# Three stage boundaries reordered: first rows normalised in halves on two engines, then two weight tiles multiplied chunk by chunk

## What is computed

```
def rmsnorm(x, g):
    xf = x.astype(jnp.float32)
    y = xf * lax.rsqrt(jnp.mean(xf * xf, axis=-1, keepdims=True) + EPS)
    return (y * g.astype(jnp.float32)).astype(x.dtype)

    h = modulate(rmsnorm(x, ffn1_pre_g[l]), m[0], m[1])          # stage ffn1
    y = swiglu(h, ffn1_w_gate[l], ffn1_w_up[l], ffn1_w_down[l])
    x = x + 0.5 * m[2][:, None, :] * rmsnorm(y, ffn1_post_g[l])

    h = modulate(rmsnorm(x, mix_pre_g[l]), m[3], m[4])           # stage mix1
    proj = h @ w_in[l]
    ...
    x = x + m[5][:, None, :] * rmsnorm(y, mix_post_g[l])

    h = modulate(rmsnorm(x, ffn2_pre_g[l]), m[6], m[7])          # stage ffn2
    y = swiglu(h, ffn2_w_gate[l], ffn2_w_up[l], ffn2_w_down[l])
    x = x + 0.5 * m[8][:, None, :] * rmsnorm(y, ffn2_post_g[l])
```

## Time and profile before

| | us |
|---|---|
| median of three runs | 2482.9 |
| the runs | 2482.52, 2482.9, 2487.58 |
| time of the profiled execution | 2484.59 |
| its span in the trace | 2482.8 |
| PE busy | 2442.2 (98% of the span) |
| DVE busy | 1613.1 (65%) |
| ACT busy | 1206.1 (49%) |
| POOL busy | 681.8 (27%) |

### The profile page before, as it was taken

One profiled execution on the slowest core, in us unless ns is written; L12 is line 12 of the kernel. 1 busy time (PEld: TensorE's weight loads), 2 busy tenths in 40 slices (PEclk: granted clock), 3 DMA queues, 4 the chain that ended last, 5 costly groups with the idle time before them and its releaser, 6 DMA issues.

```text
span 2482.8 us, 40495 instructions
## 1 busy us (share of the span) xinstructions
PE 2442.2 (98%) x16435; PEld 2242.0 (90%) x16435; DVE 1613.1 (65%) x3096; ACT 1206.1 (49%) x1828; POOL 681.8 (27%) x326
## 2 busy tenths in 40 slices
PE   8999989999999999999999999999999999999999
PEld 8997869988989999999888888889999999888887
DVE  7777866647556568999444445574676899644444
ACT  5444664446644454434444445664444434444443
POOL 1210001112036560000444443115662000344443
PEclk9999999999999999999999999999999999999999
DMA  9996436654355554444656655335555444556554
GB/s 349 404 336 241 136 111 196 203 195 150 119 165 176 171 179 148 142 139 138 212 191 195 195 192 196 123 115 193 184 170 164 143 137 144 186 189 196 192 195 161
DMA packets 126732, 457.45 MB, mean 184 GB/s; under 512 B 14117, under 2 KB 17105, under 8 KB 125778
## 3 DMA queue, kind: packets, MB, share of 16 engines
q1 hardware_dynamic: 121858, 442.57, 53.6%
q10 hardware_dynamic: 4048, 8.91, 1.1%
q0 software_dynamic: 640, 3.37, 0.4%
HBM read 451.63 MB, written 5.93 MB: 184 GB/s over the span
## 4 chain that ended last, share of the span: by engine, by line
PE 84%; DVE 2%; ACT 1%; POOL 0%; issue 0%; ACTq 0%
PE bank L612 25%; PE bank L614 25%; PE bank L613 25%; PE bank L1199 4%; PE bank L979 1%; PE bank L1170 1%; PE bank L840 1%; DVE sb L1870 0%; PE bank L1122 0%; PE bank L627 0%; ACT sb L1242 0%; PE bank L997 0%; DVE sb L1931 0%; PE bank L829 0%; POOL sb L2783 0%; PE bank L1084 0%
## 5 line engine op out<-in xcount | busy, mean ns | idle before, releaser
L612 PE MATMUL bank<-sb,sb 128*128 128x256 f32 (+1 forms) x4744 | 1518.9, 320 | 12.4 <-DVE sb L1870 4.5
L613 PE MATMUL bank<-sb,sb 128*128 128x256 f32 (+1 forms) x4744 | 1493.5, 315 | 0.0
L614 PE MATMUL bank<-sb,sb 128*128 128x256 f32 (+1 forms) x4744 | 1493.3, 315 | 0.0
L1242 ACT ACTIVATE sb<-sb 128x1024 fp32r<-128x1024 f32 x765 | 809.4, 1059 | 1162.6 <-PE bank L614 1143.5
L1870 DVE TENSOR_TENSOR sb<-sb,sb 128x1024 fp32r<-128x1024 f32 x511 | 628.4, 1231 | 584.8 <-ACT sb L1242 582.4
L2771 POOL TENSOR_TENSOR sb<-sb,sb 128x1024 fp32r<-128x1024 f32 x254 | 623.0, 2454 | 1325.5 <-ACT sb L1242 1321.5
L612 PEld LDWEIGHTS bank<-sb,sb 128*128 128x128 f32 x4744 | 907.8, 191 | 77.1 <-issue 12.6
L613 PEld LDWEIGHTS bank<-sb,sb 128*128 128x128 f32 x4744 | 908.6, 192 | 55.1 <-issue 1.0
L614 PEld LDWEIGHTS bank<-sb,sb 128*128 128x128 f32 x4744 | 907.5, 191 | 55.6
L2735 DVE TENSOR_TENSOR sb<-sb,sb 128x1024 fp32r<-128x1024 f32 x64 | 159.9, 2498 | 149.5 <-ACT sb L1826 149.5
L2698 DVE TENSOR_SCALAR sb<-sb,sb 128x128 f32<-128x128 f32 x512 | 142.5, 344 | 0.0
(11 more groups left out here) (274 smaller groups left out, 1199.7 us busy)
## 6 DMA issues: line engine op xcount, KB each, us to landing
sb<-in_peer_down_dram SPq DMA_DIRECT2D x256, 512.0 KB, 3.3
sb<-in_peer_up_dram SPq DMA_DIRECT2D x256, 512.0 KB, 3.3
sb<-in_w_ada_dram SPq DMA_DIRECT2D x72, 512.0 KB, 7.5
sb<-in_hyb_in_dram SPq DMA_DIRECT2D x56, 512.0 KB, 3.4
sb<-in_ffn_gate_dram SPq DMA_DIRECT2D x44, 512.0 KB, 4.8
sb<-in_ffn_up_dram SPq DMA_DIRECT2D x44, 512.0 KB, 4.6
sb<-in_ffn_down_dram SPq DMA_DIRECT2D x44, 512.0 KB, 4.2
sb<-in_mix_in_dram SPq DMA_DIRECT2D x25, 512.0 KB, 3.4
```

What stands on the lines that cost most here:

```text
L612: e.matmul(out, a[0], b[0], start=start, stop=False)
L613: e.matmul(out, a[0], b[1], start=False, stop=False)
L614: return e.matmul(out, a[1], b[0], start=False, stop=stop)
L1242: self.e.activation(rr(M.hi[k % NSPLIT]), M.raw[k % NRAW], AF.Copy).then_inc(*self.S.tick("hi", k))
```

## The change

It touches the three gated boundaries, and in one detail the order of the transposes everywhere.

- **DVE, `gated_residual`:** the first half of the rows t = 0 is normalised ahead of `times(1, 1)` and `add(1)`; the second half isn't done on DVE any more.
- **ACT, `gated_residual`:** a new `normalise` does that second half in the place of one of the three splits; the first of the later splits follows it. The third split (tile 2) moves: into `shifted`, behind chunk 1, at the entry to mix1 and ffn2; in front of the features at hyb0.
- **ACT and DVE, `shifted`:** for the odd chunks ACT writes `hhi` itself by a second read of the bank; DVE copies only the even ones.
- **`LOWS`:** the low part of tile 1 of mix1 and ffn2 is made by POOL and no longer by DVE.
- **PE, `features`:** the rows t = 0 are transposed in the order 0 to 7 (before: 0, 4, 1, 5, ...), k of 4 and more waiting for ACT's half. At mix1 and ffn2 follows one matmul over a single row, 512 columns, plain float32 (`opened`), which sets the first pair's bank to zero; then the rows t = 1.
- **PE, `first_pair`:** tiles 0 and 1 are multiplied together into that bank: chunks 0 to 3 of tile 0, chunks 0 to 3 of tile 1, then chunk 4 of both, chunk 5 of both, and so on.

```
@@ LOWS
-    "mix1": ((33, ("dve",)),),
+    "mix1": ((1, ("dve",)), (2, ("pool",)), (33, ("dve",))),
@@ Tensor
     def features(self):
...
+        banks = [self.take() for _ in range(4)]
+        for t in range(2):
+            for k in (0, 4, 1, 5, 2, 6, 3, 7) if t else range(8):
+                self.after_rows(t, k)
+                o = 256 * (k // 4) + 128 * t
+                x = self.e.transpose(banks[k % 4][:, o:o + 128], M.xn[:, t, 128 * k:128 * (k + 1)], M.const("ident"))
+                if t and k >= 4:
+                    x.then_inc(*self.S.tick("turned", s, "x", k % 4))
+            if t == 0 and s and shifted:
+                self.first = self.opened()
...
+    def opened(self):
+        M, bank = self.M, self.take()
+        o = M.consts["upto"][0]
+        self.e.matmul(bank, M.const("later")[0:1, :], M.con[0:1, o:o + 512], start=True, stop=False)
+        return bank
+
+    def first_pair(self, name, *freed):
+        M, bank = self.M, self.first
+        self.K.bank[name] = bank
+        tiles = [self.taken() for _ in range(2)]
+        for i, c in [(i, c) for i in range(2) for c in range(4)] + [(i, c) for c in range(4, 8) for i in range(2)]:
+            hi, lo = self.weights(tiles[i])
+            self.after_low(tiles[i])
+            self.wait_ge("h_lo", self.s, "x", c)
+            w = slice(128 * c, 128 * (c + 1))
+            x = self.mm3(bank[:, 256 * i:256 * (i + 1)], (hi[:, w], lo[:, w]), (rr(M.hhi[:, c]), rr(M.hlo[:, c])),
+                         False, i == 1 and c == 7)
+            if c == 7:
+                x.then_inc(*self.S.tick("tile", tiles[i]))
...
@@ Scalar, shifted
-        for dst in (self.m.f[k % 4],) if s else (self.m.f[k % 4], rr(M.hhi[:, k])):
+        for dst in (self.m.f[k % 4], rr(M.hhi[:, k])) if s == 0 or k % 2 else (self.m.f[k % 4],):
@@ Scalar, features
             self.shifted(k)
+            if self.s and k == 1:
+                self.ahead()
@@ Scalar, gated_residual
         square(1, 1)
-        self.split()
+        self.normalise(s + 1)
         self.split()
         self.squares(s + 1, 1)
         self.split()
+    def normalise(self, s):
+        M, c = self.M, slice(512, 1024)
+        self.wait_ge("rstd", s, "x", 0)
+        self.e.activation(M.xn[:, 0, c], M.x[:, 0, c], AF.Copy, scale=self.norm_of(s, "x_r0")).then_inc(*self.S.tick("xn_act", s))
@@ Vector, shifted
         for k in range(8):
             self.wait_ge("feature", s, "x", k)
-            self.e.tensor_copy(rr(M.hhi[:, k]), f[k % 4]).then_inc(*self.mark())
+            if k % 2 == 0:
+                self.e.tensor_copy(rr(M.hhi[:, k]), f[k % 4]).then_inc(*self.mark())
             copied.append(self.n_own)
             if k != 1:
                 rest(k - 1 if k else 0)
@@ Vector, gated_residual
         mean(1)
+        self.normalise(s + 1, 0, (0,))
         times(1, 1)
         add(1)
-        self.normalise(s + 1, 0)
         self.root(s + 1, 1)
         self.normalise(s + 1, 1)
```

More of the change, by code:

```diff
@@ L559, in gate_counts, with after_rows @@
         return 0 if n < 64 else n - 63 if n < 126 else 64
+    def after_rows(self, t, k):
+        if t == 0 and k >= 4 and self.s and kind_of(STAGES[self.s - 1]) in ("ffn", "mix"):
+            self.wait_ge("xn_act", self.s)
+        else:
+            self.wait_ge("xn", self.s, t, k // 4)
     def after_xn(self):
@@ L634, in features @@
     def features(self):
-        M = self.M
+        M, s = self.M, self.s
         shifted = kind_of(self.name) in ("ffn", "mix")
-        self.transposes("x", lambda t, k: M.xn[:, t, 128 * k:128 * (k + 1)], list(range(8)),
-                        lambda t, k: ("xn", self.s, t, k // 4),
-                        lambda k: ("feature", self.s, "x", k) if shifted else ("h_lo", self.s, "x", k))
-        if self.s:
-            self.ahead()
+        banks = [self.take() for _ in range(4)]
[8 more added lines that the diff above has]
+                self.first = self.opened()
+        for b in range(4):
+            self.K.bank["turned", s, "x", b] = banks[b]
+            self.give(banks[b], ("feature" if shifted else "h_lo", s, "x", b + 4))
+        if s:
+            self.ahead()
+    def opened(self):
[16 more added lines that the diff above has]
+                x.then_inc(*self.S.tick("tile", tiles[i]))
+        for _ in tiles:
+            self.used()
+        self.give(bank, *freed)
     def linear_T(self, out):
@@ L786, in ffn @@
             self.tasks["bias"] = self.lines()
-        for j in range(NFF):
+        if self.s:
+            self.first_pair(("hidden", self.s, 0), ("hidden", self.s, 0))
+        for j in range(1 if self.s else 0, NFF):
             bank = self.take()
@@ L907, in mix @@
         self.tasks = {"rows": self.rows(), "recurrence": self.recurrence(), "attention": self.mix_attention()}
-        for i in range(2):
-            self.pair(("qi", i), [("mix_qi", i)])
+        self.first_pair(("qi", 0), ("mix_qi", 0))
+        self.pair(("qi", 1), [("mix_qi", 1)])
         self.pair(("ki",), [("mix_ki",)], 1)
@@ L1293, in features @@
     def features(self):
+        shifted = kind_of(self.name) in ("ffn", "mix")
+        if self.s and not shifted:
+            self.ahead()
         if self.s:
-            self.ahead()
             self.fence()
         for k in range(8):
-            if kind_of(self.name) in ("hyb", "peer"):
+            if not shifted:
                 break
@@ L1918, in root, with normalise @@
         self.mean(s, "x", t, self.norm_of(s, f"x_ss{t}", 2))
-    def normalise(self, s, t):
+    def normalise(self, s, t, halves=(0, 1)):
         M = self.M
@@ L1924, in normalise @@
         self.wait_ge("rstd", s, "x", t)
-        for m in range(2):
+        for m in halves:
             c = slice(512 * m, 512 * (m + 1))
```

2 lines of the change are left out of this document (1 added, 1 removed).

## The result

The changed kernel takes 2488.06 us at the median of 20 runs (2485.97 to 2490.99), the kernel before 2484.77 in the runs beside them (2482.41 to 2487.63, also 20). The ratio is 1.0013, with a 95% interval of 1.0007 to 1.0019: slower by 3.3 us, less than the 5 us that I had set as the bound. The prediction had said 2.9 us more than before, at 2485.8, with a range of 2481.5 to 2490.5. The kernel before, over these 20 runs, lies 1.9 us above the median of its first three (2482.9), from which I had started; this is why 2488.06 lies 2.3 above the forecast time while the difference is 0.4 off.

The account below looks back on a forecast made before the run. PE bounds (2442.2 of 2482.8 us busy); P, from the end E of the stage before's last product to PE's start on tile 2, changes +1.7 mix1, +0.2 ffn2, +0.9 hyb0, +2.9 in all: 2482.9 + 2.9 = 2485.8, range 2481.5 to 2490.5.

Parts of the forecast that it names:

- First rows earlier: Gated boundaries: transposes of rows t = 0 start at E+1.45, not E+3.53; 2.1 earlier, worth nothing by itself.
- Second rows later, +0.27: Gated boundaries: DVE work queued behind the early normalisation moves rows t = 1 by +0.27 (bounds 0 and 0.44).
- The opening matmul: Between the transposes of t = 0 and t = 1: 1.12, up to 2.2 at half clock; costs nothing, 0.1 at most.
- Features: ACT's 12 writes plus the split of tile 2 make the last chunk ready 1.5 later than E+12.43.
- POOL's low part, "E+8.7, with 3.3 in hand": Low part of tile 1 on POOL: starts after E+5.9, takes 2.8, ready E+8.7, needed at E+12.0.
- The hole of 1.8 behind one unit: PE stands still 1.8 after its first unit: chunk 0 ready at E+7.8, chunk 1 at E+10.0.
- The clock: Falls in PE's thin stretch E+5.9 to 10.5, returns E+12.1 to 16.2; P at mix1 and ffn2 17.5, not 16.3.
- hyb0, +0.9: Entry to hyb0: +0.4 for a later start, +0.5 for the clock coming back later; bounds -0.8 to +1.4.
- the clock that holds: Rival, chance 0.20: shorter idle pieces keep PE's clock at 1.00; in all -1.3, or 2481.6.
- the clock low over the whole pair: Rival, chance 0.17: clock not back before tiles 0 and 1 end, P = 19.9; in all +8, or 2490.9.
- ACT hides what I count: Rival, chance 0.06: ACT's second bank read far cheaper than 0.47, P 13.7; in all -5.7, or 2477.
- It does nothing: Rival, chance 0.07: the gate of rows t = 1 isn't shortened, gains and losses cancel; 2482.9.

Follow-up runs that it names:

- e4_old_gate: Changed kernel with the first rows normalised as before, both halves on DVE behind add(1); +3.6 us against the kernel before, ratio 1.0015.
- e2_late_split: Changed kernel with ACT's split of tile 2 behind chunk 7 and no longer behind chunk 1; +2.9 us against the kernel before, ratio 1.0017.
- e1_low_dve: Changed kernel with the low part of tile 1 of mix1 and ffn2 back on DVE; +2.2 us against the kernel before, ratio 1.0014.
- e3_both: Changed kernel with tile 1's low part back on DVE and ACT's split of tile 2 behind chunk 7; +0.4 us against the kernel before, ratio 1.0006.
- e11_pair_again: Second measurement of the kernel before with tiles 0 and 1 multiplied chunk by chunk, its gate, splits and copies kept; -2.0 us against the kernel before, ratio 0.9993.
- e12_full_after: Changed kernel with filling matmuls over all 128 rows around the transposes at the gated boundaries; -0.8 us against the kernel before, ratio 1.0003.
- e6_fill_before: Kernel before with three one-row filling matmuls ahead of the 16 transposes at each gated boundary; -0.6 us against the kernel before, ratio 0.9998.
- e9_full_before: Kernel before with three filling matmuls over all 128 rows ahead of the transposes at each gated boundary; -2.4 us against the kernel before, ratio 0.9995.
- e7_pair_fill: Kernel before with tiles 0 and 1 chunk by chunk, plus one-row filling matmuls in the gaps; +0.6 us against the kernel before, ratio 1.0005.
- e8: Kernel before with only tiles 0 and 1 multiplied chunk by chunk, its gate, splits and copies kept; -1.9 us against the kernel before, ratio 0.9994.
- e5_fill_after: Changed kernel with more one-row opening matmuls, ahead of, between and behind the transposes; +5.3 us against the kernel before, ratio 1.0027.

## Why the prediction was right, and where it wasn't

The sum was right: +2.9 against +3.3 measured, P near 17.5 against 17.43 and 17.98. (Its three terms add up to 2.8, and the sum over P in the profiles was 2.1: +1.6, +0.7 and -0.2 where I had +1.7, +0.2 and +0.9.) Part of that is luck, since steps inside it were wrong and made up for each other. At full clock I had P = 16.3 at mix1; from the first product at E+9.87 sixteen units without a gap give 15.6. The low clock should have added 1.2 and added 1.7, six units of 0.28.

- *First rows earlier, worth nothing:* right. Transposes at E+1.47 (1.45 forecast). ACT's normalisation took 0.72 and not 0.62, without effect.
- *Second rows later, +0.27:* ACT's first feature at E+6.30, not 6.41; +0.16 against before. In the lower half of its bounds.
- *The opening matmul:* 1.12 and hidden, right in the changed kernel; e4_old_gate shows the 2.07 that it costs as soon as the clock is low and its cover gone.
- *Features:* the chain on ACT was as worked out; its last write ended at E+12.8 (13.1 forecast), the last chunk was ready at E+13.6 (13.95). But it was not what bound: PE had no gap behind its first unit, since it started late and worked at half clock. e2_late_split doesn't settle this, as DVE's late copy kept the chain there almost as long; e1_low_dve and e3_both show what the split costs once that copy is in time.
- *POOL's low part, "E+8.7, with 3.3 in hand":* this is the step that failed. It took 3.26 us and not 2.8, ended at E+9.1 and was in time as data. I had asked only when the result was needed, and not what the instruction would do to DVE beside it. It held DVE's copy of chunk 0 for 2.1 us, and with it the first product (e1_low_dve: 9.87 to 7.80). I had read that POOL took 5.66 for two beside DVE, so the sign was there, with the sharing seen from POOL's side alone: the 244 subtractions of this kind in the kernel before take 2.44 in the mean.
- *The hole of 1.8 behind one unit:* not there in the changed kernel, since chunk 0 was as late as chunk 1. It came out at 1.18 in e1_low_dve. Both delays lie side by side, and the sum took only one. That is why P was near.
- *The clock:* it fell, but at E+3.6 and E+4.9, before the thin stretch from E+5.9 on in which I had it fall, and came back at E+13.8 and E+15.1, within the 12.1 to 16.2. So PE ran its second transposes at half clock too. The ungated boundary was a poor measure: there too the clock fell in two other profiles, with the same idle 1.18 ahead (e11_pair_again at 712.7, e12_full_after at 717.9, for 3.4 us each), so "it never fell" held for one profile only. The opening matmul was to cut PE's idle time in two; by e6_fill_before one-row matmuls do little for the clock. The low share of P was six to eight units of 0.28 more, about as reckoned.
- *hyb0, +0.9:* measured -0.24. The start was +0.16 (0.4 forecast: the transposes ended at E+7.55, as worked out, but the first product starts 0.1 ahead of their recorded end, as it had before); the low stretch was 3.4 and not 6.8, in this and in three of the experiments with the same gate. The step that failed is the clock that "comes back later": it fell later and so was back earlier against the products.
- *The rivals:* the clock that holds didn't happen; the clock low over the whole pair neither, at mix1 six of 16 units were low, at ffn2 eight. "ACT hides what I count" is out: its writes took 0.47 each again, and in e1_low_dve DVE waits 1.62 for them. "It does nothing" is out by the interval, 1.0007 to 1.0019.

The Trainium skill (SBUF — State Buffer, Who interferes with whom) says that a copy or cast of VectorE can enter a mode that needs the port pair it shares with GpSimd, and that whoever issues first holds the pair for its whole instruction while the other is blocked. The traces agree: 2.37, 2.32, 2.36 and 1.55 us for a copy of 0.28, each ending 0.15 to 0.2 after POOL's subtraction. What the prediction cites from the same skill (TensorE: Matmul & The Clock Gate, Part 4: PE-mode transpose) the runs don't bear out. In e9_full_before 16 transposes with short gaps passed at full clock, and in e6_fill_before and e7_pair_fill the clock rose from 1.2 to 2.4 GHz at E+7.0 and E+6.6 at mix1, behind a low stretch in which PE had run nothing but transposes. The measurement decides; the forecast's numbers didn't use it.

What stays open: how much of the 3.3 us is the clock's and how much the gates', since they aren't independent. Taking both gate causes away gives back 1.7 by the ratios and 2.9 by the medians (e3_both), holding the clock 2.5 and 4.1 (e12_full_after), and each of these carries an error of some 2.

The profiles say more, one execution each. Where the clock held, P was 15.71 with the gates of before (mix1 in e9_full_before) and 15.95 with those of the changed kernel (ffn2 in e12_full_after), so 0.2 apart. Where it was low until E+15.1, at ffn2 in the two kernels compared, P was 17.26 and 17.98, so 0.7 apart. And at mix1, where the change cost 1.6, the low stretch ended at E+9.7 before, when PE had to wait for its chunks anyway, and at E+13.8 after, in products that follow each other without a gap. This is no accident of one profile: at mix1 it ended between E+6.6 and E+9.7 in before and e6, e7, e8 and e11, and between E+13.6 and E+15.9 in the changed kernel and e1 to e5. So by these profiles most of the loss at mix1 is low clock on the products. Why it lasts longer there isn't shown: bringing the first product forward by 2.07 didn't shorten it (e1_low_dve).

Whether it is the rows or the data by which full-height matmuls hold the clock wasn't separated either: the one-row form multiplied zeros.

## What to carry to other kernels

When work moves to GpSimd, look at what VectorE does in the same 3 us: here a copy within SBUF waited for the rest of GpSimd's instruction, and a result that is "in time" can still cost its length elsewhere. Where two delays lie side by side, undo them together before calling either harmless. And price whatever is put into a gap of TensorE at half clock as well: in e4_old_gate, e5_fill_after and e7_pair_fill the clock had fallen before it ran. Last, ask at which clock the stretch runs that a change makes the bound: at mix1 a low stretch until E+9.7 cost next to nothing while PE waited for its chunks (P 15.84, and 15.71 with the clock held), and 0.28 a unit once it didn't wait.
